# Weights loaded and added in halves of a unit, each half on a semaphore of its own, in a two-layer hybrid decoder trunk

## The chip, the cores and the metric

The kernel runs on one core of a Trainium2 chip. The metric is the device time of one launch in microseconds (us), the median of several runs.

## The reference

Two layers over 256 tokens of width 1024, in float32; each has two half-step SwiGLU blocks (width 2816) around a mixing block with three branches.

```python
def reference(x, mem, ...):
    for l in range(DEPTH):
        h = rmsnorm(x, norm_ffn1[l])
        x = x + 0.5 * swiglu(h, ffn1_w1[l], ffn1_w3[l], ffn1_w2[l])

        h = rmsnorm(x, norm_mix[l])
        proj = h @ w_in[l]
        rq, rk, rv, rg, sq, sk, sv, mq, gl = jnp.split(proj, SPLIT_POINTS, axis=-1)
        ret = retention(...)                       # 4 heads, two chunks of 128
        ret = rmsnorm(ret, ...).reshape(B, S, RET_V_W) * jax.nn.silu(rg)
        swa = sliding_window_attention(...)        # 16 query heads, 2 kv heads, window 128
        mkv = rmsnorm(mem, norm_mem[l]) @ w_mem_kv[l]
        mo = memory_attention(...)                 # 4 heads over 256 memory tokens
        gates = jax.nn.sigmoid(gl.reshape(B, S, N_BRANCH, D))
        merged = (gates[:, :, 0] * (ret @ w_up_ret[l])
                  + gates[:, :, 1] * (swa @ w_up_swa[l])
                  + gates[:, :, 2] * (mo @ w_up_mem[l]))
        x = x + merged @ w_o[l]

        h = rmsnorm(x, norm_ffn2[l])
        x = x + 0.5 * swiglu(h, ffn2_w1[l], ffn2_w3[l], ffn2_w2[l])
    return rmsnorm(x, norm_final)
```

## The kernel before

All weights stand in DRAM as one `stream` of units. A unit is 128 partitions x 2048 float32, 1 MB, one row of 8 KB in each partition. TensorE multiplies in three passes of fp32r: a weight is split into a high part `w_hi` (ScalarE, L1250, a copy that rounds) and a low part `w_lo` (VectorE, L1671, the raw weight minus the high part), and the passes are x_lo*w_hi (L815), x_hi*w_hi (L816) and x_hi*w_lo (L818).

The work is a written-out list of items, 330 in all, in an order that every engine follows. An item is a unit (`u1.1`, `us1.1`: a unit of a plain projection) or one product of a pair (`p0:5`, `mq:4`). A pair takes two projections together by Strassen's scheme: seven products instead of eight, four of them on weights that are the sum or difference of two quarters. Such a weight sum is made in the raw buffer, either by VectorE (L1663, `raw_x<-raw_x,raw`) or by a DMA that GpSimd issues and that adds the second quarter in flight (L740, `accum_op=ALU.add`); the table `ADDED` says which. There are 55 such adds.

The way of a weight is: SyncE loads the unit into a raw place (L704: three places `raw`, and `raw_b`, `raw_q`, `raw_x`, `raw_a` in memory that is free for a time); perhaps a second quarter is added; ScalarE makes w_hi in two halves of 1024 columns (`PARTS`), counting `hi_split`; VectorE makes w_lo in two halves, counting `weights_made`; TensorE waits for `weights_made` and multiplies. w_hi and w_lo have three slots (a fourth, `w_hi_more`, in the SwiGLU blocks). The two splits are already made and waited for by halves; the loads and the adds are not. SyncE waits until VectorE has made the last half of the item that held the raw place (`until`, a value of `weights_made`; for the first items `first_lo`), issues one DMA of 1 MB, and that DMA's landing raises `raw_loaded[s]`. ScalarE waits for it, or, where the item's weight is a sum, for `quarter_added` or `weights_made`. All engines run in order, so whatever an engine waits for holds up all that is behind it.

At the very start the first two units come in pieces of 256 KB (L682), and the next five 1 MB loads are issued without a wait behind them.

Names used below: `act_g` is the gated SwiGLU product (VectorE, L1740), which TensorE transposes (L876); `junk` is the sum of squares (L1232), `hF` the normed input in float32 (L1283); `half` a product that is combined with a kept one `snap` (L1784); `stA` the evacuated last product of the pair mq (ScalarE, L1489); `mqT` the transposed memory queries copied out by ScalarE (L1499); `us1` the second half of the sliding-window branch's up-projection.

Of the kernel before, what the change touches and what calls it, by code (L numbers as in the profile page):

```python
# [393 lines left out]
def build(nc, x_in, mem_in, memt_in, stream, gains_in, gfin_in, rot_in, decay_in, mask_in, ident_in, out):  # L394
# [6 lines left out]
    with ctx:  # L401
# [107 lines left out]
        def sem(name):  # L509
            return ctx.enter_context(nc.semaphore(name))  # L510

        raw_loaded = [sem(f"raw_loaded{s}") for s in range(RAW_A + 1)]
        hi_split, weights_made, unit_used = sem("hi_split"), sem("weights_made"), sem("unit_used")
        x_copied, S_made, S_hi_split, S_lo_split = map(sem, ["x_copied", "S_made", "S_hi_split", "S_lo_split"])
        S_step, x0_copied = sem("S_step"), sem("x0_copied")
        quarter_added = {m: [sem(f"quarter_added{m}_{n}") for n in range(2)] for m in (5, 6, 7, 4)}
        x_stored, x_back, mkT_stored, mkT_back, mv_stored, mv_back = map(
            sem, ["x_stored", "x_back", "mkT_stored", "mkT_back", "mv_stored", "mv_back"])
        minus_ready, gated = map(sem, ["minus_ready", "gated"])
# [93 lines left out]
        def pair_no(l, f, k):  # L613
            return l * (len(PAIRS[1]) + len(PAIRS[2])) + (f - 1) * len(PAIRS[1]) + k

        def sum_ready(l, pair, k):
            if k in added(l, pair):
                turn, count = (added_at[l, pair, k] - 1) % 2, (added_at[l, pair, k] + 1) // 2
                return quarter_added[k][turn], 16 * count
            return weights_made, sum_at[l, pair, k]  # L620

        def made(l, f, k, n):
# [50 lines left out]
        def _(sp):  # L673
            def x_part(n):
                cols = X_PARTS[n]
                sp.dma_start(x[:, :, cols], x_in[:, cols].rearrange("(t p) d -> p t d", p=P)).then_inc(x_loaded[n], 16)

            x_part(0)
            for u in range(EARLY):
                for j in range(SUBS):  # L680
# [5 lines left out]
                    x_part(2)  # L686
            for o, unit, s, (until, owner), _ in loads[EARLY:]:
                if until > 0:
                    sp.wait_ge(weights_made, until)
                elif until == 0:  # L690
                    sp.wait_ge(first_lo, (owner + 1) * SUBS)
                item = item_of(o)
                again = owner is not None and o // NI == owner // NI and part_of(item_of(owner)) == part_of(item)
                if s in (*RAW_B, *RAW_Q) and part_of(item) == 2 and not again:
                    sp.wait_ge(*full(o // NI, "mg1_1"))
                if s in RAW_B and part_of(item) == 0 and not again:
                    sp.wait_ge(*full(o // NI, "mv0t1"))
                    sp.wait_ge(*full(o // NI, "mv1t1"))
                if s == RAW_A and (owner is None or o // NI != owner // NI):
                    sp.wait_ge(*full(o // NI, "mkt_3"))  # L700
                if s == RAW_X and (owner is None or o // NI != owner // NI):
                    sp.wait_ge(x_stored, 16 * (o // NI + 1))
                    sp.wait_ge(*full(o // NI, "xt1_1"))
                sp.dma_start(raw_slot(s), stream[unit]).then_inc(raw_loaded[s], 16)  # L704
            sp.wait_ge(final_ready, 1)
            sp.dma_start(out[0:P, 0:BLK], stB[:, 0, 0:BLK]).then_inc(out_stored[0], 16)
            sp.wait_ge(act_final, 1)
# [8 lines left out]
        def _(pool):  # L716
# [15 lines left out]
            def add_quarters(o):  # L732

                for l, pair, m, behind in added_after[o]:
                    to = raw_of[l, pair, WEIGHT[m]]
                    pool.wait_ge(raw_loaded[to[0]], 16 * to[1])
                    if behind:
                        pool.wait_ge(weights_made, behind)
                    _, f, k = pair
                    pool.dma_start(raw_slot(to[0]), stream[l * NU + quarter_unit(f, k, SUMS[m])], accum_op=ALU.add)\  # L740
                        .then_inc(quarter_added[m][(added_at[l, pair, m] - 1) % 2], 16)

            def quarters_after(l, i):
                if ITEMS[l][i] == ("down", 2, DOWNS[l, 2][-1]):
# [477 lines left out]
        def _(act):  # L1222
# [11 lines left out]
            def split(o):  # L1234

                l, item = o // NI, item_of(o)
                s, loads_so_far = loaded(o)
                if item[0] == "prod" and item[3] in SUMS:
                    act.wait_ge(*sum_ready(l, item[:3], item[3]))
                else:  # L1240
                    act.wait_ge(raw_loaded[s], 16 * loads_so_far)
                if slot_before[o] >= 0:
                    act.wait_ge(*used(slot_before[o]))
                if slot_of[o] == RING and item[1] == 2:
                    act.wait_ge(*full(l, "mg1_1"))
                if whole(o):
                    nc.scalar.activation(slots(o)[0][:, :], raw_slot(s)[:, :], ACT.Copy).then_inc(hi_split, 2)
                    return
                for part in PARTS:
                    nc.scalar.activation(slots(o)[0][:, part], raw_slot(s)[:, part], ACT.Copy).then_inc(hi_split, 1)  # L1250

            def splits(l, i):
# [393 lines left out]
        def _(dve):  # L1646
# [7 lines left out]
            def split(o):  # L1654

                (hi, lo), (s, _) = slots(o), loaded(o)
                for pair, m in sums_first[o]:
                    to, plus = (raw_of[o // NI, pair, q] for q in (WEIGHT[m], SUMS[m]))
                    dve.wait_ge(raw_loaded[to[0]], 16 * to[1])
                    dve.wait_ge(raw_loaded[plus[0]], 16 * plus[1])  # L1660
                    if sum_behind[o // NI, pair, m]:
                        dve.wait_ge(weights_made, sum_behind[o // NI, pair, m])
                    nc.vector.tensor_tensor(raw_slot(to[0]), raw_slot(to[0]), raw_slot(plus[0]), ALU.add).then_inc(weights_made, 1)  # L1663
# [485 lines left out]
```

## Time and profile before

| | |
|---|---|
| median of 3 runs | 1435.11 us (1435.1 to 1437.61) |
| the profiled execution | 1435.34 us |
| its span in the profile | 1433.5 us |
| TensorE busy | 1415.2 us, 99% |
| VectorE busy | 1205.6 us, 84% |
| ScalarE busy | 982.2 us, 69% |
| weight stream and the rest, mean | 234 GB/s |

The span runs from the first instruction to the end of the last; the profiled execution's own time is 1.84 us longer. "PE" is TensorE, "DVE" VectorE, "ACT" ScalarE, "POOL" GpSimd, "SP" SyncE; a q behind the name is the engine's queue of DMA issues and waits. Times in rows of the trace are counted from the span's start. A row's duration of a matmul is longer than its share of the engine, since matmuls are pipelined.

### The profile page before, as it was taken

What the parts mean: (1) busy time and instruction counts of PE and PEld (TensorE: products, weight loads), DVE (VectorE), ACT (ScalarE), POOL (GpSimd) and SP (SyncE); (2) the same over time, 40 slices, a digit from 0 to 9 for tenths busy, and PEclk for the clock granted to TensorE, in tenths of its full rate; (3) what the DMA queues carried; (4) which work ended last, traced back from release to release, by engine and by line L of the source; (5) the groups of instructions that cost most, each with busy time, mean ns of one, the idle gap of its engine ahead of it and who ended that gap; (6) DMA issues with size and microseconds to landing.
All of it is one profiled execution on the core that took longest, in us unless ns stands there. A gap on an engine that the chain in (4) does not pass through costs nothing.

```text
span 1433.5 us, 17418 instructions
## 1 busy us (share of the span) xinstructions
PE 1415.2 (99%) x6630; PEld 1161.0 (81%) x6630; DVE 1205.6 (84%) x1423; ACT 982.2 (69%) x1438; POOL 63.3 (4%) x88
## 2 busy tenths in 40 slices
PE   8999999999999999999999999999999999999997
PEld 6788888877878888888888888887778788888886
DVE  7999756889899868899889997468998898699885
ACT  6677666878766748676577675667786766576773
POOL 0000000000100000000000000000001000000000
PEclk9999999999999999999999999999999999999999
DMA  9799448787777576889749767468878765857971
GB/s 369 235 268 291 189 157 289 226 240 209 217 227 256 185 294 245 240 272 276 247 155 285 247 195 263 171 241 261 237 208 223 250 220 187 322 151 250 314 225 44
DMA packets 48675, 336.14 MB, mean 234 GB/s; under 512 B 5488, under 2 KB 6128, under 8 KB 8528
## 3 DMA queue, kind: packets, MB, share of 16 engines
q1 hardware_dynamic: 37536, 259.80, 48.4%
q0 software_dynamic: 8192, 58.59, 21.5%
q10 hardware_dynamic: 2864, 16.64, 2.9%
q8 instruction: 52, 0.85, 0.2%
q14 instruction: 31, 0.25, 0.0%
HBM read 327.67 MB, written 7.34 MB: 234 GB/s over the span
## 4 chain that ended last, share of the span: by engine, by line
PE 89%; DVE 6%; DMA 2%; ACT 1%; issue 1%; SPq 0%; POOLq 0%; POOL 0%; DVEq 0%; ACTq 0%
PE bank L815 27%; PE bank L818 27%; PE bank L816 27%; PE bank L876 3%; DVE w_lo L1671 3%; DMA raw<-in_stream 2%; PE bank L1170 1%; PE bank L1149 1%; PE bank L1031 1%; PE bank L1045 1%; ACT w_hi L1250 1%; DVE raw_x L1663 1%; PE bank L1060 1%; DVE raw_q L1663 0%; DVE w_lo_more L1671 0%
## 5 line engine op out<-in xcount | busy, mean ns | idle before, releaser
L1671 DVE TENSOR_TENSOR w_lo<-raw,w_hi 128x1024 fp32r<-128x1024 f32 x328 | 386.2, 1221 | 104.3 <-ACT w_hi L1250 103.9
L1250 ACT ACTIVATE w_hi<-raw 128x1024 fp32r<-128x1024 f32 x328 | 328.5, 1054 | 141.0 <-PE bank L818 115.5
L815 PE MATMUL bank<-w_hi,hT_lo 128*128 128x512 f32 (+1 forms) x640 | 251.4, 393 | 3.3 <-ACT stA L1489 1.6
L818 PE MATMUL bank<-w_lo,hT_hi 128*128 128x512 f32 (+1 forms) x640 | 246.2, 385 | 0.0
L816 PE MATMUL bank<-w_hi,hT_hi 128*128 128x512 f32 (+1 forms) x640 | 246.1, 384 | 0.0
L815 PE MATMUL bank<-w_hi,S_lo 128*128 128x512 f32 x400 | 158.8, 397 | 0.9 <-ACT snap L1338 0.9
L818 PE MATMUL bank<-w_lo,S_hi 128*128 128x512 f32 x400 | 155.9, 390 | 0.0
L816 PE MATMUL bank<-w_hi,S_hi 128*128 128x512 f32 x400 | 155.9, 390 | 0.0
L815 PEld LDWEIGHTS bank<-w_hi,hT_lo 128*128 128x128 f32 x640 | 120.3, 188 | 32.0 <-issue 4.0
L818 PEld LDWEIGHTS bank<-w_lo,hT_hi 128*128 128x128 f32 x640 | 120.3, 188 | 24.4
L816 PEld LDWEIGHTS bank<-w_hi,hT_hi 128*128 128x128 f32 x640 | 120.5, 188 | 22.3
L815 PE MATMUL bank<-w_hi,bT_lo 128*128 128x512 f32 x320 | 125.7, 393 | 0.0
L818 PE MATMUL bank<-w_lo,bT_hi 128*128 128x512 f32 x320 | 124.6, 389 | 0.0
L816 PE MATMUL bank<-w_hi,bT_hi 128*128 128x512 f32 x320 | 124.6, 389 | 0.0
L815 PE MATMUL bank<-w_hi,gT_lo 128*128 128x512 f32 x256 | 100.5, 393 | 0.0
L818 PE MATMUL bank<-w_lo,gT_hi 128*128 128x512 f32 x256 | 99.7, 390 | 0.0
L816 PE MATMUL bank<-w_hi,gT_hi 128*128 128x512 f32 x256 | 99.6, 389 | 0.0
L1671 DVE TENSOR_TENSOR w_lo<-raw_b,w_hi 128x1024 fp32r<-128x1024 f32 x78 | 92.0, 1222 | 7.7 <-ACT w_hi L1250 7.6
L1250 ACT ACTIVATE w_hi<-raw_b 128x1024 fp32r<-128x1024 f32 x78 | 78.2, 1054 | 21.9 <-PE bank L818 15.8
L1671 DVE TENSOR_TENSOR w_lo<-raw_q,w_hi 128x1024 fp32r<-128x1024 f32 x76 | 89.5, 1221 | 4.2 <-ACT w_hi L1250 4.1
L815 PEld LDWEIGHTS bank<-w_hi,S_lo 128*128 128x128 f32 x400 | 75.1, 188 | 18.8 <-ACT snap L1338 1.6
L1671 DVE TENSOR_TENSOR w_lo<-raw_x,w_hi 128x1024 fp32r<-128x1024 f32 x60 | 70.7, 1221 | 22.6 <-ACT w_hi L1250 22.6
(232 smaller groups left out, 2529.6 us busy)
## 6 DMA issues: line engine op xcount, KB each, us to landing
raw<-in_stream SPq DMA_DIRECT2D x154, 1024.0 KB, 5.5
raw_b<-in_stream SPq DMA_DIRECT2D x35, 1024.0 KB, 6.9
raw_q<-in_stream SPq DMA_DIRECT2D x33, 1024.0 KB, 7.7
raw<-in_stream POOLq DMA_DIRECT2D x24, 1024.0 KB, 8.7
raw_x<-in_stream SPq DMA_DIRECT2D x16, 1024.0 KB, 5.2
raw_b<-in_stream POOLq DMA_DIRECT2D x10, 1024.0 KB, 10.8
raw_q<-in_stream POOLq DMA_DIRECT2D x9, 1024.0 KB, 9.0
raw_a<-in_stream SPq DMA_DIRECT2D x6, 1024.0 KB, 5.1
```

The source lines that it names most:

```text
L815: nc.tensor.matmul(dst, xl, wh[:, a:b], start=first, stop=False, skip_group_check=more)
L816: nc.tensor.matmul(dst, xh, wh[:, a:b], start=False, stop=False, skip_group_check=more)
L818: return nc.tensor.matmul(dst, xh, wl[:, a:b], start=False, stop=last, skip_group_check=more)
L876: last = nc.tensor.transpose(bank(name)[:, at:at + P], src(t, k0 + j), ident[:, :])
L1031: last = nc.tensor.matmul(bank(name)[:, i * n:(i + 1) * n], sqT[rows, head // 2, tokens(b)], skT[rows, head // (SWA_H // SWA_KV), 0:n], st ...
L1045: last = nc.tensor.transpose(bank(name)[:, i * P:(i + 1) * P], prob[:, g % 2, head, part * P:(part + 1) * P], ident[:, :])
L1060: nc.tensor.matmul(o, v, heads[:, :, odd, 0:2, :], start=True, stop=False, skip_group_check=True)
L1149: last = nc.tensor.matmul(bank(name)[:, t * MEM:(t + 1) * MEM], mqT[:, 2 * h + k, tokens(t)], mkT[:, 2 * h + k, :], start=k == 0, stop=k == 1)
L1170: last = nc.tensor.matmul(bank(name)[:, j * SEQ:(j + 1) * SEQ], mv[:, m, k * P:(k + 1) * P], mpT[:, h, m, :], start=m == 0, stop=m == 1)
L1250: nc.scalar.activation(slots(o)[0][:, part], raw_slot(s)[:, part], ACT.Copy).then_inc(hi_split, 1)
L1663: nc.vector.tensor_tensor(raw_slot(to[0]), raw_slot(to[0]), raw_slot(plus[0]), ALU.add).then_inc(weights_made, 1)
L1671: nc.vector.tensor_tensor(lo[:, part], raw_slot(s)[:, part], hi[:, part].bitcast(F32), ALU.subtract)\
```

## The change

Every load of L704 becomes two DMAs of 512 KB, columns 0 to 1023 and 1024 to 2047 of the unit, so rows of 4 KB instead of 8 KB. Every raw place has two semaphores, one for each half. Where the place's last reader is a split, SyncE issues the first half when VectorE has made the first half of that reader's w_lo (`until - 1`), and waits for the second only before the second half's DMA; where the last reader is a sum, both halves wait for the sum as before. ScalarE waits for each half before that half's w_hi. GpSimd's adds become two each (110 in all), each waiting for its own half of the loaded place and both for the same count of `weights_made` as before. VectorE's sums wait for both halves of both places. The pieces of L682 are not touched.

```diff
-        raw_loaded = [sem(f"raw_loaded{s}") for s in range(RAW_A + 1)]
+        raw_loaded = [[sem(f"raw_loaded{s}_{n}") for n in range(2)] for s in range(RAW_A + 1)]
-        quarter_added = {m: [sem(f"quarter_added{m}_{n}") for n in range(2)] for m in (5, 6, 7, 4)}
+        quarter_added = {m: [[sem(f"quarter_added{m}_{n}_{h}") for h in range(2)] for n in range(2)] for m in (6, 7, 4)}
...
+            SPLIT_ENDS = {v for v in lo_at if v}
...
                 if until > 0:
-                    sp.wait_ge(weights_made, until)
+                    sp.wait_ge(weights_made, until - (until in SPLIT_ENDS))
...
-                sp.dma_start(raw_slot(s), stream[unit]).then_inc(raw_loaded[s], 16)
+                for n, part in enumerate(PARTS):
+                    if n and until > 0 and until in SPLIT_ENDS:
+                        sp.wait_ge(weights_made, until)
+                    sp.dma_start(raw_slot(s)[:, part], stream[unit, :, part]).then_inc(raw_loaded[s][n], 16)
...
-                    pool.wait_ge(raw_loaded[to[0]], 16 * to[1])
-                    if behind:
-                        pool.wait_ge(weights_made, behind)
                     _, f, k = pair
-                    pool.dma_start(raw_slot(to[0]), stream[l * NU + quarter_unit(f, k, SUMS[m])], accum_op=ALU.add)\
-                        .then_inc(quarter_added[m][(added_at[l, pair, m] - 1) % 2], 16)
+                    for h, part in enumerate(PARTS):
+                        pool.wait_ge(raw_loaded[to[0]][h], 16 * to[1])
+                        if behind:
+                            pool.wait_ge(weights_made, behind)
+                        pool.dma_start(raw_slot(to[0])[:, part], stream[l * NU + quarter_unit(f, k, SUMS[m]), :, part], accum_op=ALU.add)\
+                            .then_inc(quarter_added[m][(added_at[l, pair, m] - 1) % 2][h], 16)
...
-                if item[0] == "prod" and item[3] in SUMS:
-                    act.wait_ge(*sum_ready(l, item[:3], item[3]))
-                else:
-                    act.wait_ge(raw_loaded[s], 16 * loads_so_far)
+                def raw_there(h):
+                    if item[0] != "prod" or item[3] not in SUMS:
+                        act.wait_ge(raw_loaded[s][h], 16 * loads_so_far)
+                    elif item[3] in added(l, item[:3]) or h == 0:
+                        act.wait_ge(*sum_ready(l, item[:3], item[3], h))
+
+                raw_there(0)
...
-                for part in PARTS:
+                for n, part in enumerate(PARTS):
+                    if n:
+                        raw_there(1)
                     nc.scalar.activation(slots(o)[0][:, part], raw_slot(s)[:, part], ACT.Copy).then_inc(hi_split, 1)
...
-                    dve.wait_ge(raw_loaded[to[0]], 16 * to[1])
-                    dve.wait_ge(raw_loaded[plus[0]], 16 * plus[1])
+                    for n in range(2):
+                        dve.wait_ge(raw_loaded[to[0]][n], 16 * to[1])
+                        dve.wait_ge(raw_loaded[plus[0]][n], 16 * plus[1])
```

No engine's compute instructions move. What moves is seen at two places. First SyncE's queue at the start of the program, behind the pieces of L682 (`raw`, `raw_b`, `raw_q` are the raw places). Before:

```order
L704 DMA raw<-in_stream 128x2048
L704 DMA raw_b<-in_stream 128x2048 x2
L704 DMA raw_q<-in_stream 128x2048 x2
L704 DMA raw<-in_stream 128x2048 [waits first_lo] x2
L704 DMA raw<-in_stream 128x2048 [waits weights_made]
```

And now:

```order
L709 DMA raw<-in_stream 128x1024 x2
L709 DMA raw_b<-in_stream 128x1024 x4
L709 DMA raw_q<-in_stream 128x1024 x4
L709 DMA raw<-in_stream 128x1024 [waits first_lo]
L709 DMA raw<-in_stream 128x1024
L709 DMA raw<-in_stream 128x1024 [waits first_lo]
L709 DMA raw<-in_stream 128x1024
L709 DMA raw<-in_stream 128x1024 [waits weights_made] x2
```

Five loads without a wait have become ten; the first pair is the third item's weight. Second, ScalarE's splits in layer 1's mixing block; the rows with `unit_used` are those of the item us1.1. Before:

```order
L1250 ACTIVATE w_hi<-raw 128x1024 [waits unit_used,raw_loaded2]
L1250 ACTIVATE w_hi<-raw 128x1024
L1250 ACTIVATE w_hi<-raw 128x1024 [waits psum_full1,quarter_added4_0]
L1250 ACTIVATE w_hi<-raw 128x1024
L1250 ACTIVATE w_hi<-raw 128x1024 [waits psum_full0,raw_loaded0]
L1250 ACTIVATE w_hi<-raw 128x1024
```

And now:

```order
L1261 ACTIVATE w_hi<-raw 128x1024 [waits unit_used,raw_loaded2_0]
L1261 ACTIVATE w_hi<-raw 128x1024 [waits raw_loaded2_1]
L1261 ACTIVATE w_hi<-raw 128x1024 [waits psum_full1,quarter_added4_0_0]
L1261 ACTIVATE w_hi<-raw 128x1024 [waits quarter_added4_0_1]
L1261 ACTIVATE w_hi<-raw 128x1024 [waits psum_full0,raw_loaded0_0]
L1261 ACTIVATE w_hi<-raw 128x1024 [waits raw_loaded0_1]
```

Each half of a split has its own wait. GpSimd's queue shortly ahead of that place issues the adds of the products mq:7 and mq:4. Before:

```order
L740 DMA raw<-in_stream 128x2048 [waits weights_made,raw_loaded1]
L727 TENSOR_TENSOR rstd_r<-msq_r,eps 128x8 [waits retsq_ready]
L730 TENSOR_TENSOR rstd_r<-rstd_r,mhalf 128x8 [waits pool_step]
L740 DMA raw_x<-in_stream 128x2048 [waits weights_made,raw_loaded7]
L740 DMA raw<-in_stream 128x2048 [waits weights_made,raw_loaded1]
```

And now:

```order
L746 DMA raw<-in_stream 128x1024 [waits weights_made,raw_loaded1_0]
L746 DMA raw<-in_stream 128x1024 [waits weights_made,raw_loaded1_1]
L732 TENSOR_TENSOR rstd_r<-msq_r,eps 128x8 [waits retsq_ready]
L735 TENSOR_TENSOR rstd_r<-rstd_r,mhalf 128x8 [waits pool_step]
L746 DMA raw_x<-in_stream 128x1024 [waits weights_made,raw_loaded7_0]
L746 DMA raw_x<-in_stream 128x1024 [waits weights_made,raw_loaded7_1]
L746 DMA raw<-in_stream 128x1024 [waits weights_made,raw_loaded1_0]
L746 DMA raw<-in_stream 128x1024 [waits weights_made,raw_loaded1_1]
```

Each add has become two in a row, with GpSimd's own small steps between the same adds as before.

## Rows read from the trace of the kernel before

**Rows 1.** The page: busy time, share of the span, instructions.
```profile
PE 1415.2 (99%) x6630; PEld 1161.0 (81%) x6630; DVE 1205.6 (84%) x1423; ACT 982.2 (69%) x1438; POOL 63.3 (4%) x88
```

**Rows 2.** Waits of TensorE: us in total, times, longest us.
```profile
PE bank L876 <- DVE act_g L1740: 2.3, 1, 2.3
...
PE bank L815 <- DVE half L1784: 1.7, 2, 1.5
PE bank L815 <- ACT snap L1338: 1.6, 3, 0.7
PE bank L815 <- ACT stA L1489: 1.6, 2, 0.8
PE bank L876 <- ACT mqT L1499: 0.9, 2, 0.6
```

**Rows 3.** The chain of waits, 0 to 75 us: start, us, what.
```profile
7.01 9.43 DMA raw<-in_stream
...
27.87 0.79 DVE act_g L1740 x2
...
69.35 0.61 DVE half L1784
```

**Rows 4.** The timeline of ScalarE at the start; in brackets its idle time.
```profile
13.60 2.20 ACT L1261 ACTIVATE w_hi<-raw 128x512 fp32r<-128x512 f32 x4
16.46 2.01 ACT L1250 ACTIVATE w_hi<-raw 128x1024 fp32r<-128x1024 f32 x2 [0.66 <-DMA raw<-in_stream]
```

**Rows 5.** The timeline of TensorE where it waits, up to 72 us.
```profile
28.91 0.63 PE L876 MATMUL bank<-ident,act_g 128*128 128x128 f32 x4 [2.32 <-DVE act_g L1740]
...
70.00 0.50 PE L815 MATMUL bank<-w_hi,hT_lo 128*128 128x512 f32 x1 [1.46 <-DVE half L1784]
```

**Rows 6.** The chain of waits in layer 1's mixing block.
```profile
396.06 9.71 DMA raw<-in_stream
...
420.92 2.30 DVE raw_x L1663
423.24 2.01 ACT w_hi L1250 x2
```

**Rows 7.** The timelines of ScalarE and VectorE there, and ScalarE in layer 2.
```profile
405.80 5.80 ACT L1250 ACTIVATE w_hi<-raw 128x1024 fp32r<-128x1024 f32 x6 [5.77 <-DMA raw<-in_stream]
...
406.89 2.36 DVE L1671 TENSOR_TENSOR w_lo<-raw,w_hi 128x1024 fp32r<-128x1024 f32 x2 [1.55 <-ACT w_hi L1250]
...
1123.16 0.69 ACT L1489 ACTIVATE stA<-bank,rstd 128x512 f32<-128x512 f32 x1 [0.24 <-PE bank L818]
```

**Rows 8.** The timeline of TensorE in the two mixing blocks.
```profile
408.42 0.39 PE L818 MATMUL bank<-w_lo,S_hi 128*128 128x512 f32 x1
408.64 0.39 PE L815 MATMUL bank<-w_hi,bT_lo 128*128 128x512 f32 x1
...
417.74 0.50 PE L815 MATMUL bank<-w_hi,hT_lo 128*128 128x512 f32 x1 [0.78 <-ACT stA L1489]
...
425.87 0.30 PE L876 MATMUL bank<-ident,stB 128*128 128x128 f32 x1 [0.60 <-ACT mqT L1499]
...
1131.70 0.41 PE L876 MATMUL bank<-ident,stB 128*128 128x128 f32 x2 [0.28 <-ACT mqT L1499]
```

**Rows 9.** DMA issues: times, KB each, median us to landing.
```profile
raw<-in_stream SPq DMA_DIRECT2D x154, 1024.0 KB, 5.5
...
raw<-in_stream POOLq DMA_DIRECT2D x24, 1024.0 KB, 8.7
```

**Rows 10.** The two adds at 388.9 and 391.2 us (line L740).
```profile
L740 POOL DMA_DIRECT2D raw_x<-in_stream x1: 898/898/898, 388.9 to 388.9; - x1
...
DMA to landing us min/median/max: 8.0/10.8/13.6
```

**Rows 11.** Busy time by stretch; last are PEclk, DMA share, GB/s.
```profile
8.00:13.00 5.00, 4.89 (x25) 3.63 (x24) 2.98 (x6) 3.24 (x8) 0.00 (x0) 1.00 1.06 407
14.00:26.00 12.00, 11.87 (x53) 9.51 (x52) 10.01 (x16) 9.26 (x17) 2.69 (x5) 1.00 1.02 423
...
30.00:32.00 2.00, 2.00 (x7) 1.52 (x6) 2.00 (x2) 1.60 (x3) 0.00 (x0) 0.50 1.01 416
```

More of the change, by code:

```diff
@@ L614, in pair_no, with sum_ready @@
             return l * (len(PAIRS[1]) + len(PAIRS[2])) + (f - 1) * len(PAIRS[1]) + k
-        def sum_ready(l, pair, k):
+        def sum_ready(l, pair, k, h):
             if k in added(l, pair):
                 turn, count = (added_at[l, pair, k] - 1) % 2, (added_at[l, pair, k] + 1) // 2
-                return quarter_added[k][turn], 16 * count
+                return quarter_added[k][turn][h], 16 * count
             return weights_made, sum_at[l, pair, k]
```

## The prediction

> **What bounds the kernel now.** I read the page first. TensorE is busy for 1415.2 of 1433.5 us [rows 1], so a change to loads can win only what TensorE loses by waiting, 18.3 us with the start and the end of the program. The page's chain of waits seems to offer more (it gives VectorE 6% and DMAs 2% of the span), but a chain names the work that ended last before each step, not the time TensorE lost by it. So I went to the waits of TensorE [rows 2]. They are few: 2.3 us for `act_g`, 1.7 for `half`, 1.6 for `snap`, 1.6 for `stA`, 0.9 for `mqT`. None is for `w_lo`: the split weights are always there in time, although loads take 5.5 us at the median and adds 8.7 [rows 9]. What the change can win is what late raw weights do at second hand: they hold up ScalarE and VectorE, whose queues also carry `act_g`, `half` and `mqT`. So I looked at the chain ahead of each of those waits.
>
> **Start.** The chain begins with a load issued at 7.01 us, which lands 9.43 us later [rows 3]. ScalarE starts its split at 16.46 after 0.66 us of idle time [rows 4]; from there ScalarE and VectorE have no pause that matters up to `act_g` at 27.87, for which TensorE waits at 28.91 (2.32 us idle), and on to `half` at 69.35, which ends its wait at 70.00 [rows 3, 5]. In between nothing but VectorE's backlog sets the pace.
>
> **Mixing block.** In layer 1 the chain runs from a load issued at 396.06 that takes 9.71 us [rows 6]. ScalarE was idle for 5.77 us until it landed, VectorE for 1.55 us until ScalarE had the first half of w_hi, at 406.89 [rows 7]. VectorE works on without a pause to the sum `raw_x` at 420.92; ScalarE splits that at 423.24, and behind it in its queue stands `mqT`, for which TensorE waits at 425.87 (0.60 us) and in layer 2 at 1131.70 (0.28 us) [rows 6, 8].
>
> **The change, part by part.**
>
> *The third item's load, in halves: -0.7 us.* From 8 to 26 us the DMA engines are full, 407 to 423 GB/s [rows 11], so 512 KB takes 0.524 MB / 423 GB/s = 1.24 us, and the first half should land at about 16.4 - 1.2 = 15.2 us. ScalarE is busy with the pieces until 13.60 + 2.20 = 15.80 [rows 4]. It then starts at 15.8 instead of 16.46, its second half (15.8 + 1.0) finds the second half of the load landed at about 16.4 to 16.5, and the whole chain moves by 0.66 us. An instruction that need not wait may start a little before the end of the one ahead, so I take 0.7. TensorE gets it once, at 70.00: what it gains earlier it waits for there.
>
> *The load at 396.06, in halves.* Its first half is issued when VectorE has made half of the reader's w_lo, 1.2 us earlier, and has half the bytes. Ahead of it stand two adds, issued at 388.95 and 391.22, one of which takes 13.6 us to land [rows 10]; they are what makes 9.71 us of a load that takes 5.5 at the median. Pessimistically the second half still lands at 405.8 and only the first is early. Then ScalarE has the first half of w_hi ready and makes the second at 405.8 instead of one instruction (1.0 us, half of the 2.01 [rows 4]) later, and VectorE gains about 1.0 us. Optimistically both are early, and VectorE gains all 1.55 us of its idle time [rows 7]. Either is more than TensorE waits for `mqT`. Those waits cost 0.60 and 0.28 us of idle time, and the refilling of the pipeline 0.16 more each (matmuls in a row start 0.22 us apart, though each lasts 0.39 [rows 8]): 0.76 + 0.44 = **-1.2 us** for both layers. The range for this term is 0 to -1.2, since no more can be won than is waited.
>
> *The waits for `stA` at 417.74 and in layer 2 stay.* They stand on the same chain, and one might count them too. But `stA` reads the bank that TensorE has just finished: in layer 2 ScalarE waits 0.24 us for TensorE before it starts at 1123.16 [rows 7], so the 0.78 us is TensorE to ScalarE and back. The same holds for `snap`.
>
> *Halves as such.* Rows of 4 KB instead of 8: the trace has loads with rows of 2 KB (the pieces and x, 8 to 13 us, 407 GB/s) and of 8 KB (14 to 26 us, 423 GB/s) [rows 11]. If the rate fell with the row to 407, a load would be 4% longer, 0.1 us of 2.5. It is hidden behind the distance that w_lo has from its use. Nearest to being late is us1.1: VectorE ends its first half at 406.89 + 1.22 = 408.11 and TensorE uses it at 408.64, 0.5 us later [rows 7, 8], and this is the item that the change brings forward. The doubled issues cost SyncE and GpSimd time that they have: GpSimd is busy 63.3 us in all [rows 1], and 55 more adds at 0.9 us each [rows 10] make 50. The second half of an add is issued 0.9 us after the first, while that one's transfer still runs. ScalarE's and VectorE's extra waits are for semaphores long raised; I take nothing for them, and if a wait cost 0.05 us, the four sums on VectorE's path up to 70 us would give 0.4 us back.
>
> *Sum.* 1435.34 - 0.7 - 1.2 = 1433.4 us for an execution like the profiled one; that one lies 0.2 above the median, so **1433.2 us**.
>
> **A rule against it.** The half-add is what the trace does not show. For all bytes of an add to be fixed cost is excluded by nothing here; what is seen is an add at 8.7 us beside a load of the same size at 5.5 [rows 9]. Between the ends (3.2 us fixed for each half, or nothing) I take nothing, because five loads issued in a row at the start move at 423 GB/s [rows 11], so that whatever is fixed lies beside the other transfers. The Trainium skill (DMA: Bandwidth & Descriptors, "Measured (HBM→SBUF, 128 partitions, SWDGE, issued from GpSimd)") gives the rule to batch DMAs to at least 1 MiB, and its section on the anatomy of one DMA a fixed cost of about 2.0 us each. By that rule, with nothing overlapped, two adds ahead of the load would take 4 us more, and us1.1 would come some 3 us late in each layer: about 1439.
>
> **Rivals.**
> - *Nothing comes of it* (15%). The halves share the queues with the adds and land together, or another wait takes over at once: 1435.1. For it: the load's 9.71 us come from adds that move the same bytes as before [rows 6, 10]. Against it: ScalarE needs only half the bytes to begin, and at the start the queue is a plain row of loads.
> - *More comes of it* (7%). The waits for `stA` go too, 2 x 0.94 us: 1431.3. Against it is the 0.24 us that ScalarE waits for TensorE.
> - *The clock takes it back* (6%). After the idle 2.32 us at 28.91 the granted clock falls to 0.50, which is 1.2 GHz, in 30 to 32 us [rows 5, 11]; after the idle 1.46 us at 70.00 it does not. If the first wait becomes 1.6 us and the clock stays at 2.4 GHz, TensorE is some 1.6 us ahead (an estimate: about 3 us at half clock, of which the row shows 2, give back half of it) and must wait that much longer at or before 70 us, because VectorE sets the pace there. A fall of the clock behind that longer wait would cost about 1.6 us: 1434.8.
> - *Slower: half-adds cost nearly what whole ones cost* (10%). Place: the two adds ahead of the load at 396.06. With 3.2 us fixed for each extra half, 6.4 us more stand ahead of it. The second half has 1.2 us (its own earlier issue or size) and TensorE 0.6 us of slack, so it begins to cost above 0.9 us per extra half; at 3.2 us it is 6.4 - 1.8 = 4.6 us a layer, 9.2 in all, less 0.7 at the start: 1443.6. For it: the adds are 3.2 us longer than loads. Against it: a transfer that moves twice the data must be longer by the byte.
>
> **How the numbers follow.** The forecast has 62% and its own range 1432.3 to 1434.2: the start gives 0.3 to 0.8, the mixing blocks 0.6 to 1.2, and the median wanders by some tenths. 0.2%, or 2.9 us, is about what a measurement of this kernel can tell from no change. So the forecast counts as the same, except for some 4% of its own spread; faster is that and the second rival, 11%; slower is the last rival, 10%; the same is 79%. The range reaches from the second rival to a small version of the last, 1431.0 to 1436.5 us.
>
> **What the profile afterwards would show.** ScalarE's first split of 1024 columns at 15.7 to 15.8 us without idle time; TensorE's wait at 28.91 shorter by 0.7 and at about 28.2; the pass at 70.00 at about 69.3; the item us1.1's first w_hi several us before 405.8, VectorE's idle time of 1.55 us ahead of it gone; no wait for `mqT` in either layer; the waits for `stA` unchanged at 0.78. Loads of 512 KB at 3.5 to 4.5 us and half-adds at 5.5 to 6.5. The prediction is wrong if a wait for `w_lo` appears among TensorE's, if half-adds take over 8 us, or if the clock is low in another stretch than 30 to 34 us.

## The result and the profile after

The changed kernel takes 1438.37 us at the median of 12 runs (1437.25 to 1441.69), the kernel before 1435.18 (12 runs, 1434.27 to 1437.85) on the same chip. The ratio is 1.0021, 95% interval 1.0014 to 1.0029: slower by about 3 us, where I forecast 2 us less and gave a range that ends at 1436.5. A ratio is taken over all runs of both kernels, so it is not just that of the two medians. The profiled execution took 1439.15 us, its span is 1437.4.

The waits of TensorE after the change, of the same view as [rows 2] (us in total, times, longest):

```profile
PE bank L821 <- DVE half L1796: 2.6, 3, 1.4
PE bank L821 <- DVE gates L1913: 2.1, 2, 1.4
...
PE bank L821 <- DVE S_lo L1734: 1.6, 2, 1.0
PE bank L882 <- DVE act_g L1752: 1.6, 1, 1.6
PE bank L821 <- ACT stA L1500: 1.6, 2, 0.8
...
PE bank L882 <- DVE gT_lo L1701: 0.8, 1, 0.8
PE bank L882 <- ACT mqT L1510: 0.5, 1, 0.5
```

`act_g` is down from 2.3 to 1.6 and `mqT` from 0.9 to 0.5, as hoped. What is new is `gates` (the gates of the three branches, ahead of their sigmoid, VectorE) with 2.1 us, `gT_lo` (the low part of the transposed `act_g`) with 0.8, `S_lo` (the low part of the input sums that pair products use) with 1.6, and a third wait for `half`. The two for `S_lo`, at 43.17 and 47.11, cost nothing: TensorE only comes there earlier. I put the two traces side by side at the same instructions of TensorE. At the start the kernel after is ahead (timelines of ScalarE and TensorE; compare [rows 4, 5]):

```profile
15.35 2.02 ACT L1261 ACTIVATE w_hi<-raw 128x1024 fp32r<-128x1024 f32 x2
...
27.82 0.63 PE L882 MATMUL bank<-ident,act_g 128*128 128x128 f32 x4 [1.58 <-DVE act_g L1752]
...
68.90 0.50 PE L821 MATMUL bank<-w_hi,hT_lo 128*128 128x512 f32 x1 [1.44 <-DVE half L1796]
```

68.90 against 70.00 is 1.1 us gained. Then TensorE meets waits that it did not have before (its timeline, later stretches):

```profile
109.53 0.63 PE L882 MATMUL bank<-ident,act_a 128*128 128x128 f32 x4 [0.81 <-DVE gT_lo L1701]
121.49 0.50 PE L821 MATMUL bank<-w_hi,S_lo 128*128 128x512 f32 x1 [0.42 <-DVE half L1796]
...
426.39 2.03 PE L882 MATMUL bank<-ident,stB 128*128 128x128 f32 x16 [0.48 <-ACT mqT L1510]
440.95 0.50 PE L821 MATMUL bank<-w_hi,S_lo 128*128 128x512 f32 x1 [1.44 <-DVE gates L1913]
...
1147.79 0.50 PE L821 MATMUL bank<-w_hi,S_lo 128*128 128x512 f32 x1 [0.69 <-DVE gates L1913]
```

At 426.39 it is 0.52 us behind (425.87 in [rows 8]), at 440.95 2.04 us, at 1147.79 2.99, and its last matmul starts 2.97 us later (1428.31 against 1425.34). The spans differ by 3.9; the other 0.9 us lie behind TensorE's last matmul. Against the same instructions before, TensorE loses 0.97 us at 109.53, 0.58 at 121.49, 1.52 at 440.95, 0.54 at 710.69 (another wait for `gT_lo`) and 0.72 at 1147.79. So the start's gain of 1.1 us is gone by 121.49. Ahead of 109.53 stands an add of which ScalarE makes the first half and then waits for the second, which lands at 106.44; the whole add landed at 102.69, when ScalarE wasn't ready for it (after, then before):

```profile
106.46 1.06 ACT L1261 ACTIVATE w_hi<-raw_q 128x1024 fp32r<-128x1024 f32 x1 [2.20 <-DMA raw_q<-in_stream]
...
104.33 2.00 ACT L1250 ACTIVATE w_hi<-raw_q 128x1024 fp32r<-128x1024 f32 x2
```

The largest single step is that at 440.95. The chain of waits there is short, and it begins with the second half of the add for the pair `gr`, quarter 7:

```profile
426.54 0.53 POOL raw L746
427.07 10.82 DMA raw<-in_stream
...
437.92 1.07 ACT w_hi L1261
...
440.16 0.75 DVE gates L1913
```

ScalarE and VectorE do the first half at 433.48 and 434.69, and then stand still in the middle of the item, 3.29 and 3.11 us, because each goes through its queue in order and the second half is not there:

```profile
437.92 2.95 ACT L1261 ACTIVATE w_hi<-raw 128x1024 fp32r<-128x1024 f32 x3 [3.29 <-DMA raw<-in_stream]
439.01 1.23 DVE L1683 TENSOR_TENSOR w_lo<-raw,w_hi 128x1024 fp32r<-128x1024 f32 x1 [3.11 <-ACT w_hi L1261]
```

In the kernel before, the same place looked harmless, since no wait of TensorE is listed there. I had not looked at it. Its rows (ScalarE, VectorE, TensorE, kernel before):

```profile
434.75 3.90 ACT L1250 ACTIVATE w_hi<-raw 128x1024 fp32r<-128x1024 f32 x4 [1.59 <-DMA raw<-in_stream]
...
438.12 0.75 DVE L1901 SCALAR_TENSOR_TENSOR gates<-bank,minus_rstd,snap_late 128x512 f32<-128x512 f32 x1
...
438.61 0.39 PE L818 MATMUL bank<-w_lo,bT_hi 128*128 128x512 f32 x1
438.92 0.50 PE L815 MATMUL bank<-w_hi,S_lo 128*128 128x512 f32 x1
```

`gates` ends at 438.87 and TensorE starts at 438.92, 0.31 us after its matmul before instead of the usual 0.22: it waited 0.09 us, too little for the list. So the landing of this add (434.73) already set TensorE's time. The arithmetic closes: the add was issued at 426.02 and landed after 8.7 us; now its first half is issued at 426.54 and its second lands at 437.90, 3.2 us later. One half of the chain behind it (1.15 us) is already done by then, and 3.2 - 1.15 = 2.0 us is TensorE's delay there. In layer 2 the same holds: the add landed at 1140.6 before and its second half at 1144.7 after, TensorE passes at 1144.80 and 1147.79; 4.1 - 1.15 = 3.0.

The DMA issues and queues after the change (times, KB each, median us to landing; then packets, MB and share of 16 engines' span), beside [rows 9]:

```profile
raw<-in_stream SPq DMA_DIRECT2D x308, 512.0 KB, 6.1
...
raw<-in_stream POOLq DMA_DIRECT2D x48, 512.0 KB, 8.2
```

```profile
q1 hardware_dynamic: 72672, 259.82, 50.8%
q0 software_dynamic: 16112, 58.60, 22.4%
```

Half the bytes, and no earlier: a load of 512 KB takes 6.1 us where 1 MB took 5.5, a half-add 8.2 where a whole one took 8.7. Over all 55 adds, from the issue of the first half to the landing of the last, the mean is 11.3 us (whole adds before: 9.5); both are worked out from every issue and landing in the trace.

### The profile page after: what moved, and what is told of

Its sections match the earlier page's. It is cut to its first block, busy times and chain, and to the rows that moved or that the text cites. A ratio compares the mean times of both kernels' runs of the same rounds, so it can differ in the third digit from the quotient of the medians.

```text
span 1437.4 us, 17829 instructions
## 1 busy us (share of the span) xinstructions
PE 1414.3 (98%) x6630; PEld 1159.8 (81%) x6630; DVE 1205.0 (84%) x1423; ACT 983.1 (68%) x1438; POOL 112.2 (8%) x143
## 4 chain that ended last, share of the span: by engine, by line
PE 78%; DVE 12%; DMA 6%; issue 2%; ACT 2%; POOL 0%; DVEq 0%; POOLq 0%; ACTq 0%
PE bank L821 23%; PE bank L824 23%; PE bank L822 23%; DVE w_lo L1683 6%; DMA raw<-in_stream 3%; PE bank L882 3%; DMA raw_q<-in_stream 2%; DVE w_lo_more L1683 2%; PE bank L1155 1%; PE bank L1176 1%; PE bank L1037 1%; PE bank L1051 1%; DMA raw_b<-in_stream 1%; ACT w_hi L1261 1%; DVE raw_q L1675 1%
## 5 line engine op out<-in xcount | busy, mean ns | idle before, releaser
L1261 ACT ACTIVATE w_hi<-raw_q 128x1024 fp32r<-128x1024 f32 x76 | 76.4, 1053 | 21.4 <-DVE raw_q L1675 8.1
```

## The experiments

The kernel with whole adds is the reference for the later ones, so the two halves of the change come first.

**1 to 4. Loads and adds apart.** Adds whole again, on one semaphore, the loads as in the kernel after:

```
-  for h, part in enumerate(PARTS):
-      pool.wait_ge(raw_loaded[to[0]][h], 16 * to[1])
-      pool.dma_start(raw_slot(to[0])[:, part], stream[..., part], accum_op=ALU.add).then_inc(...[h], 16)
+  for h in range(2):
+      pool.wait_ge(raw_loaded[to[0]][h], 16 * to[1])
+  pool.dma_start(raw_slot(to[0]), stream[...], accum_op=ALU.add).then_inc(...[0], 16)
```

> The kernel after, with every add whole again on one semaphore; the loads stay in halves, the first half issued a count early. Theory A (the adds in halves lose the time: with both engines' work cut to half rows, an add's second half lands 3 to 4 us later than the whole one did, at 106.44 against 102.69 us and at 437.90 against 434.72, and ScalarE and VectorE, which go in order, stand for it): the new waits of TensorE near 109.5, 440.95 and 1147.8 us are gone, and the gains stay, -1.1 us at the start and -0.8 to -1.2 at the two waits for mqT: 1433.0 us, 1432.5 to 1434. Theory B (the loads lose it: their first half is issued earlier now, and takes turns with an add under way): the waits stay and the time is that of after, 1437.5 to 1439.

Measured: 1433.22 us, ratio to before 0.9986 (0.9978 to 0.9995). Loads whole, adds in halves:

```
-  sp.wait_ge(weights_made, until - (until in SPLIT_ENDS))
+  sp.wait_ge(weights_made, until)
-  for n, part in enumerate(PARTS): ... sp.dma_start(raw_slot(s)[:, part], ...).then_inc(raw_loaded[s][n], 16)
+  sp.dma_start(raw_slot(s), stream[unit]).then_inc(raw_loaded[s][0], 16)
```

> The kernel after, with every load whole again and issued as before; only the adds are in halves. Theory A (adds in halves): both gains are gone and the losses stay, 1438 to 1440 us. Theory B (loads): the time of before, 1435.2 within 0.5 us. A third theory, C (the two together: a load of 4 KB rows against an add of 4 KB rows is no other share than 8 KB against 8 KB, but a load in whole rows of 8 KB against an add in rows of 4 KB takes more of the shared engines than before): worse than after by more than the lost gains of 2 us, over 1440.5.

Measured: 1443.14 us, 1.0039 (1.0025 to 1.0054). The halves of a load both issued at `until`, adds in halves:

```
-  sp.wait_ge(weights_made, until - (until in SPLIT_ENDS))
+  sp.wait_ge(weights_made, until)
```

> The kernel after, with both halves of a load issued only at the count at which the whole one was issued before. Adds stay in halves. Theory A (adds in halves): losses stay, and the gain at the wait for mqT in layer 2 shrinks by at most 0.4 us; 1438 to 1439. Theory B in its form 'the first half comes too early': the losses at 109.5 and 440.95 go, 1433 to 1434.5.

Measured: 1436.85 us, 1.0013 (1.0001 to 1.0024). The same with whole adds:

> Late halves of loads and whole adds: nothing but the semaphores of the loads, and their rows of 4 KB, differ from before. Theory A: 1433 to 1434.2 us, the start's gain of 1.1 us and part of the other. Theory C's mirror (rows of 4 KB of a load against rows of 8 KB of an add give the load the smaller share): the raw halves that are loaded beside an add land later than the whole did, and the mean landing of SP's raw loads rises over the 6.1 us of after. Theory B in the form 'early' says 1434, and e1 then is 3 us above this one.

Measured: 1433.88 us, 0.9991 (0.9981 to 1.0001).

| adds | loads whole | halves, both at `until` | halves, first one early |
|---|---|---|---|
| whole | 1435.2 (before) | 1433.9 | 1433.2 |
| in halves | 1443.1 | 1436.9 | 1438.4 (after) |

With whole adds, halves of loads win 1.3 to 2.0 us (the 2.0 is clear of noise, the interval of the 1.3 ends at 1.0001); halves of adds lose 3 to 8 us whatever the loads do. Theory A stands and theory B falls as the main cause, though with half-adds the early issue came out 1.5 us above the late one, as B would have it; the runs of the late one scatter from 1435.0 to 1443.1, so I don't build on it. The 1443.1 for whole loads beside half-adds is where theory C put it, but doesn't show it: its seven runs are three from 1438.3 to 1440.3 and four from 1443.1 to 1443.4, and its adds land after 11.1 us on the mean, no later than the 11.3 of the kernel after. In its profiled execution (1443.27) TensorE waits for a `snap` behind an add whose second half lands 15.3 us after its issue, and the granted clock is low behind that wait (timeline, then the stretch with PEclk third from the end):

```profile
794.34 0.50 PE L818 MATMUL bank<-w_hi_more,S_lo 128*128 128x512 f32 x1 [2.35 <-ACT snap L1346]
```

```profile
795.00:797.00 2.00, 2.00 (x7) 1.56 (x6) 1.79 (x3) 1.18 (x2) 0.00 (x0) 0.52 0.45 94
```

The profiled execution of the late halves with half-adds (1443.10) has the same at another place: 3.72 us of wait for `gates` at 441.28, and a clock of 0.50 from 441 to 445 us and 0.52 from 445 to 447. In both kernels every execution above 1442 us has a mean granted clock of 0.996 or 0.997, every one below 1439 us 0.998 or 0.999. So the upper end of the 3 to 8 us holds some of this clock, by an estimate 1.7 us in the first and 3 in the second (the missing share of the clock, times its stretch: 795 to 799 us and 441 to 447). The waits of TensorE with loads in halves and whole adds:

```profile
PE bank L821 <- DVE half L1796: 2.2, 2, 1.4
...
PE bank L821 <- ACT stA L1500: 1.6, 2, 0.8
PE bank L882 <- DVE act_g L1752: 1.5, 1, 1.5
```

No `gates`, no `gT_lo`, no `mqT`. And TensorE passes the place of 438.92 at 436.58, the add having landed at 432.38 (issued 423.56, 8.8 us).

**5. Beside the add for `gr` 7: the loads that bring `mkT` and `mv` (the memory's keys and values, below "back-loads") back, in halves too.**

```
-  act.dma_start(mkT..., mkT_kept).then_inc(mkT_back, 16)
+  for part in PARTS:
+      act.dma_start(mkT...[:, part], mkT_kept[:, part]).then_inc(mkT_back, 16)
```

> The kernel after, with the loads that bring mkT and mv back (rows of 8 KB on ScalarE's queue, beside the add for gr:7) cut in halves of 4 KB rows as well. Theory D, shares: an engine takes one packet of each queue in turn, so a 4 KB packet of an add gets 327 ns for each 309 ns of a back-load's 8 KB packet, where a whole add's packet got 629 ns for the same; with all packets at 4 KB (some 160 ns for a back-load's) the add for gr:7 lands its second half 1 to 2 us earlier than 437.90, and the two waits of TensorE for gates (1.4 and 0.7 us) and what follows them shrink: 1435.5 to 1437.3. Theory E, a fixed cost of each DMA of an add, whatever its rows and its neighbours: nothing changes, 1438 to 1439.

Measured: 1436.33 us, 1.0005 (0.9997 to 1.0014); 2.0 us less than after. The add's second half lands 9.3 us after its own issue instead of 10.8, and the waits for `gates` are gone from the list. This is theory D's figure and not E's: nothing about the add was changed, only its neighbours. They are now two DMAs each as well as rows of 4 KB; this run doesn't part the two. In its profiled execution the wait at 109.53 is gone too, though nothing there was changed; so that wait differs between executions whatever is changed here.

**6. Two DMAs to an add, one wait.** Both halves count on one semaphore:

```
-  return quarter_added[k][turn][h], 16 * count
+  return quarter_added[k][turn][h], 32 * count
```

> The kernel after, with both halves of an add counted on one semaphore, so that ScalarE starts the first half of a raw place only when both have landed: 4 KB rows and two DMAs stay, the second wait within an item goes. Theory F, the split wait does the harm (ScalarE and VectorE, in order, stand in the middle of an item with its first half taken): 1433 to 1435. Theories D and E (the late landing does it): as after or up to 1 us worse, 1438 to 1439.5, since the second half's landing sets the end either way.

Measured: 1449.05 us, 1.0094 (1.0081 to 1.0107). Theory F is wrong in sign: the second wait within an item is not the harm, it takes away 10.7 us of it. Two DMAs instead of one cost 15.8 us (1449.05 - 1433.22), of which handing on by halves gives 10.7 back. Both figures hold some clock: three of the four runs have a mean granted clock of 0.996, and the fourth, at 0.998 and with no low stretch in its trace, took 1446.26, 13.0 us over. D and E had the sign but not the size.

**7. Two DMAs to an add, with rows of 8 KB: 64 partitions each, one wait.**

```
-  for h, part in enumerate(PARTS):
-      pool.dma_start(raw_slot(to[0])[:, part], ...
+  for h, rows in enumerate([slice(0, P // 2), slice(P // 2, P)]):
+      pool.dma_start(raw_slot(to[0])[rows], ...
```

> As the run with one wait for both halves, but the halves of an add are 64 partitions each with rows of 8 KB: two DMAs, whole packets. Theory D, shares by packet: the landing is that of a whole add within 0.5 us and the time that of the run with whole adds, 1433.2 to 1434.2. Theory E, a fixed cost of each DMA: as after, 1437.5 to 1439.

Measured: 1450.87 us, 1.0109 (1.0096 to 1.0122), and a mean landing of 11.3 us over the 55 adds, that of halves with short rows. So theory D alone is wrong: long rows don't save an add that is cut in two. (The clock is at 0.50 here as well, from 444 to 447 us in the profiled execution, so some 1.7 us of the difference are clock, an estimate.)

**8. One whole add in a layer**, that for `gr` 7, the others in halves:

```
+  if (k, m) == ("gr", 7):
+      pool.dma_start(raw_slot(to[0]), stream[...], accum_op=ALU.add).then_inc(gr_added, 16)
```

> The kernel after, with one add in a layer whole again, that for gr:7 (issued at 426 and some 1132 us), the other 53 in halves. If the loss is made at that place, where the add shares the engines with the two back-loads and its product has the least slack, 1433.8 to 1435.3; if it is spread over the adds, at most 1 us comes back, 1437.3 to 1438.4.

Measured: 1436.03 us, 1.0007 (0.9994 to 1.002). Between the two expectations: of the 5.2 us that the half-adds cost with two waits (1438.4 - 1433.2), 2.3 come back with 2 adds of 55. That the rest is spread over the others is what is left, not shown; the kernel before, measured beside each group of runs, moved by 0.8 us itself (1434.79 to 1435.58).

**9. One DMA with short rows**, one wait:

```
-  pool.dma_start(raw_slot(to[0]), stream[...], accum_op=ALU.add)
+  pool.dma_start(raw_slot(to[0]).rearrange("p (h c) -> p h c", h=2)[:, :, 0:1020],
+                 stream[...].rearrange("p (h c) -> p h c", h=2)[:, :, 0:1020], accum_op=ALU.add)
```

> The run with loads in halves and whole adds, with each add still one DMA on one semaphore but cut into rows of 4080 bytes (it leaves the last 4 of each 1024 columns of the addend out, so that two rows don't join to one). Two DMAs to an add took 15.8 us more than one (1449.0 against 1433.2, with one wait each), with rows of 4 KB or of 8 KB. If it is the number of DMAs: 1433 to 1434.5, and adds land as in that run, on a mean of 9.8 us. If it is the number of packets as well: 1438 or more, and a mean of over 11 us.

Measured: 1446.63 us, 1.0060 (1.0037 to 1.0083); its runs lie from 1436.2 to 1449.5. DMA issues, of the kernel with loads in halves and whole adds, then of this one:

```profile
raw<-in_stream POOLq DMA_DIRECT2D x24, 1024.0 KB, 8.8
raw_b<-in_stream POOLq DMA_DIRECT2D x10, 1024.0 KB, 11.0
```

```profile
raw<-in_stream POOLq DMA_DIRECT2D x24, 1020.0 KB, 9.3
raw_b<-in_stream POOLq DMA_DIRECT2D x10, 1020.0 KB, 12.1
```

The mean landing is 11.0 us against 9.8. The number of DMAs alone isn't the cause either: short rows in one DMA do much of the harm as well. How much is uncertain: in the profiled execution (1446.73) TensorE waits 3.07 us for `w_lo` at 443.04 and the clock is 0.50 from 444 to 449 us, and the two runs with the highest mean clock, 0.999, took 1436.2 and 1440.2.

**10. The adds by themselves.**

> No decoder: 48 adds one after the other, each begun when all before has landed; the output is not the reference's. Four forms (whole; two DMAs of columns; two DMAs of 64 partitions; one DMA of 4080-byte rows), each alone, beside one whole load that SP issues after it, and beside a load in halves; four times each. Time of all is of no interest; the landing of each form is. If two DMAs cost a fixed time, they land 2 to 3 us after the whole one in every setting. If the cost lies in sharing (the load begins between the two parts of the add, and takes turns with the second), they land within 0.7 us of it alone, as the adds at 577 and 1177 us of the kernels did (8.3 and 9.0 against 8.1 and 7.9), and 2 to 3 us later beside a load, while that load lands earlier by about as much as beside a whole add. By shares of packets the form of 4080-byte rows would be late beside the whole load; by number of DMAs it is not.

Each pair is the mean of four: from the first issue to the last landing of the add, and to that of the load beside it.

| form of the add | alone | beside a whole load | beside a load in halves |
|---|---|---|---|
| whole | 8.0 | 9.2, load 10.4 | 8.6, load 10.9 |
| two DMAs of columns | 8.1 | 11.3, load 11.4 | 9.8, load 11.1 |
| two DMAs of 64 partitions | 8.3 | 10.7, load 12.0 | 9.9, load 11.7 |
| one DMA, 4080-byte rows | 8.2 | 10.6, load 10.8 | 9.5, load 10.9 |

Three of its adds in rows (issue and landing, second round): whole, and columns, beside a whole load; columns alone.

```profile
L425 POOL DMA_DIRECT2D raw<-in_stream x1: 868/868/868, 167.9 to 167.9; - x1
...
DMA to landing us min/median/max: 9.1/9.1/9.1
```

```profile
L431 POOL DMA_DIRECT2D raw<-in_stream x2: 859/1034/1209, 178.8 to 179.3; - x2
...
DMA to landing us min/median/max: 5.3/7.8/10.3
```

```profile
L431 POOL DMA_DIRECT2D raw<-in_stream x2: 862/1037/1212, 142.4 to 143.0; - x2
...
DMA to landing us min/median/max: 5.6/6.6/7.7
```

There is next to no fixed cost: alone, an add in two lands 0.1 to 0.3 us after a whole one. Beside a load each cut form lands 0.9 to 2.1 us later than the whole one. The load mostly doesn't gain by it: its landing is 0.0 to 1.6 us later too, of which 0.2 to 0.9 is that it was issued later, behind the longer issue of these adds. From its own issue it gains clearly in one case, in halves beside columns (8.8 us instead of 9.4). My last expectation, that one DMA of short rows isn't late beside a whole load, is refuted (10.6 against 9.2), as run 9 had it.

**11. Only the start's loads in halves**, everything else as before:

```
+  if until <= 0: (two halves, on two semaphores)
+  else: sp.dma_start(raw_slot(s), stream[unit]).then_inc(raw_loaded[s], 16)
```

> The kernel before, with only the eight loads of the start that wait for no count of weights_made in halves with two waits; all later loads and all adds whole. The start's term by itself: -0.7 us by my prediction, -1.1 by the trace of after: 1434.0 to 1434.6. If it holds the whole of the 2.0 us that loads in halves with whole adds gained, 1433.2; then the split of the load at 396.06 was worth nothing.

Measured: 1434.95 us, 1.0005 (0.9995 to 1.0015). TensorE is 0.97 us ahead up to the mixing block, and there gives all of it back (its timeline):

```profile
425.21 2.03 PE L886 MATMUL bank<-ident,stB 128*128 128x128 f32 x16 [0.65 <-ACT mqT L1517]
438.92 0.50 PE L825 MATMUL bank<-w_hi,S_lo 128*128 128x512 f32 x1 [0.58 <-DVE gates L1921]
```

It passes at 438.92, as before. The place is set by the add, and what is gained ahead of it is lost unless that add lands earlier too. It was issued 0.64 us earlier (425.38 instead of 426.02), but took 9.35 us instead of 8.70 and landed at 434.73, as before (434.72). Its neighbours, the back-loads, were issued 0.66 us earlier too; that this is why it took longer is likely by run 5, not shown. At the end TensorE is 0.41 us ahead. The medians differ by 0.3 us, the interval holds no change, and 0.6 to 1.2 was expected.

**12. Loads in halves with one wait**, adds whole:

```
-  act.wait_ge(raw_loaded[s][h], 16 * loads_so_far)
+  act.wait_ge(raw_loaded[s][h], 32 * loads_so_far)
```

> The run with loads in halves and whole adds (1433.2), with both halves of a load counted on one semaphore, so that ScalarE starts on a raw place only when it is all there. If handing on by halves is what the loads gained: the start's 1.1 us and the wait for mqT are as in before or worse, since the second half lands some 1 us later than a whole load did, 1435.2 to 1438. If the earlier issue of the first half was the gain, 1433 to 1434. For the adds the same step (two DMAs, one wait) cost 10.6 us against two waits.

Measured: 1436.23 us, 1.0010 (1.0001 to 1.0019), 3.0 us over the run with two waits (each beside its own runs of the kernel before, +1.4 and -2.0). What loads in halves win is the handing on, not the earlier issue. For loads the handing on is worth more than the cut costs; for adds it is not.

## Why the prediction was wrong

**The step that failed** is "Halves as such", and in it the sentence "It is hidden behind the distance that w_lo has from its use". I priced a half-add at nothing, between the ends of 3.2 us and nothing, and took as evidence that five loads in a row move at 423 GB/s. Those are loads among loads, with nothing else beside them. A half-add lands 8.2 us after its issue at the median, not the 5.5 to 6.5 I wrote (over 8 was one of my signs of being wrong). From the first half's issue to the second's landing an add takes 1.8 us longer than before on the mean, 2.7 and 3.0 at the two waits for `gates`. The cost is not where the distance of w_lo could hide it: TensorE does not wait for w_lo, it waits for `gates`, `gT_lo` and `half`, which VectorE makes behind the late w_lo in its queue. `gates` is 2.2 of the 4.3 us that TensorE loses at such places. I had written that late raw weights act at second hand, and then measured the cover at first hand.

**The main place that I overlooked** is 438.92 (and 1144.80 in layer 2). I took the list of TensorE's waits for the list of places where a landing matters. It lists where time is already lost; a place where TensorE arrives 0.09 us early is as sensitive and doesn't stand there.

**Term by term.** *The start, -0.7:* -1.1 at 68.90. In the ten kernels with loads in halves and two waits TensorE passes this place 0.4 to 1.3 us earlier than in the one trace of before, 0.9 on the mean; in that with whole loads 0.4 and in that with one wait 0.6. So about 0.4 of it is no work of the halves, some 0.5 are, and my 0.7 is of the right size. *The load at 396.06, -1.2:* right with whole adds, where both waits for `mqT` are gone. After, only the second half's landing counts, 407.46 against 405.80, and 0.48 us of wait remains in layer 1; my pessimistic case, that the second half still lands at 405.8, was not pessimistic enough. (0.6 us of the 1.7 is that all there runs later by then.) *The waits for `stA` stay:* right, 0.78 us twice in nearly every run. In weighing the last rival I also put TensorE's slack at us1.1 at 0.6 us where my own rows gave 0.5. *Clock:* the granted clock at 30 to 32 us is 1.00 now (0.50 in [rows 11]). TensorE is up to 2.7 us ahead for that and waits for it at 43.17, 47.11, 61.71 and 68.90, with no fall of the clock behind these waits: that rival's first half came true, its cost did not. Where the waits grew longer (2.35 us in run 2, 3.72 in run 3) the clock did fall.

```profile
30.00:32.00 2.00, 2.00 (x11) 1.64 (x10) 2.00 (x2) 0.51 (x2) 0.00 (x0) 1.00 1.03 399
```

*Sum:* 1433.2 was forecast, and 1433.22 is what the change takes with its adds left whole. That they agree to 0.02 us is luck: the ratio's interval allows a gain of 0.7 to 3.2 us. The 5.2 us between that and the 1438.4 are the half-adds.

**The rival on the other side** named the cause (half-adds cost something) and had the wrong place and price: 3.2 us fixed for each half, at us1.1. The rule of the Trainium skill (DMA: Bandwidth & Descriptors, "Measured (HBM→SBUF, 128 partitions, SWDGE, issued from GpSimd)") to batch to 1 MiB gave about 1439 in my estimate, beside the 1438.4 measured. The number fits by luck, the mechanism as I applied it does not: alone, the second DMA costs 0.1 to 0.3 us, not 2.0. The Trainium skill has another entry (DMA: Bandwidth & Descriptors, "Rules for kernel authors") that says of two transfers to disjoint halves of the partitions that they aren't worth the bother, and to use one of 128; run 7 agrees and goes further, with 17.7 us over whole adds. I had not weighed it.

**How the time is lost.** An add shares the engines with a load or with the back-loads; by the records of the adds' packets in the trace, a whole add for `gr` 7 (kernel before) has begun some 95 of its 128 packets when the first packet of the back-loads comes at 431.9, and an add in columns (kernel after) some 140 of its 256 at 431.4. From there on the queues advance by about one packet each. The add in columns has 7.2 packets left for each of the 16 engines, the whole one 2.1, and each of them waits for one of the neighbour's. With (327 + 324) ns and (629 + 324) ns for such a pair, the median packet times there, that is 4.7 and 2.0 us, an estimate; the last packets ended 5.7 and 2.2 us after. The Trainium skill (DMA: Bandwidth & Descriptors, "Queues, rings and completion order") has engines going round the queues by packets of some nine or more descriptors each; the records here show about equal numbers of rows from both queues in that time (114 of the add and 119 of the back-loads, columns), and in the kernel before 18 and 14 rows of the add in the next two microseconds, where turns of one row each would give 17; the records name no engine, so runs of nine are not excluded on any single one. Run 10 agrees with sharing by rows. This accounts for most of what short rows cost (runs 5, 9, the columns of 10); the estimate is 1.0 us short for the columns. It doesn't account for run 7, whose rows are long. In one such add of run 10 the last three of 128 packets came alone in the last 2 us, but the records name no engine. Why two DMAs of long rows are served worse than one is open; that they are is shown in runs 7 and 10.

## What to carry to other kernels

Price a cut transfer beside its neighbours, not alone: in halves it costs nearly nothing by itself, and 1 to 2 us when other queues are at work, which a consumer gets back only if it uses the first half while the second is under way. Here that was so for loads and not for adds. So cut the transfers that start a chain (loads that an engine stands idle for), and leave whole those that must finish against others. And before pricing a delay at nothing, look past the list of waits for places where the bounding engine arrives within some tenths of a microsecond of its releaser: the interval between two matmuls (0.31 instead of 0.22) shows them, and a gain ahead of such a place is lost there too if what it waits for doesn't land earlier (run 11). Read medians beside the granted clock: behind the longest waits here it was low for some microseconds, and the kernel lost more than the wait.

## What was not expected of the hardware

- Two DMAs of 64 partitions with 8 KB rows land nearly as late as two of short rows (11.3 us beside a whole load): 10.7, where one DMA took 9.2; alone 8.3 against 8.0.
- Cutting the neighbours in two, with half the row, brought an add forward by 1.5 us (10.8 to 9.3) without touching it.
- The median landing of a 512 KB load, 6.1 us, is longer than that of a 1 MB load in the kernel before, 5.5.
- Kernels with slow adds also scatter more: 1434.8 to 1437.9 with whole adds and one wait, 1436.2 to 1449.5 with one DMA of short rows. The longest of these have the lowest mean granted clock, 0.995, the shortest 0.999.
